# Layer two's attention: output weights halved ahead of the Fourier read-out, three roots behind the last exponential, zero products in waits of both layers

## The chip, the cores and the metric

The kernel runs on one core of a Trainium2 chip. Its time is the time on the device from start to end, in microseconds (us); lower is better. The engines are TensorE (PE, with its weight loads PEld), VectorE (DVE), ScalarE (ACT), GpSimd (POOL) and SyncE (SP), which issues the DMAs. Each runs its own program in order and they meet at semaphores.

## The reference, cut to what matters

The model has two parts that run one after the other on 256 tokens of width 1024. The first part has two layers of token mixers and experts; the second has four feed-forward blocks, a recurrent block and a pooling block. The change touches the token mixers of the first part:

```
for l in range(2):
    hx, hc = modulated rms_norm of x and of the context
    px, pc = hx @ w_in, hc @ w_in
    ya = chunk_spatial_gating(...)        # group 0
    yb = fourier_mix(...)                 # group 1
    yc = softmax0(q k) - lam*softmax1(q k), times v      # group 2: "c", 4 heads
    yd = softmax(q k + bias + mask), times v             # group 3: "d", 4 heads
    y  = rms_norm over each head of [ya yb yc yd], times head gain
    x  = x + g1 * (y @ w_out)
    x  = x + g2 * expert_choice_ffn(...)  # 16 experts, 12 MB of weights each
```

Layer one (l = 0) does this for the 256 tokens and the 256 of the context, layer two (l = 1) has context only as keys and values, so it has half of the query tiles.

## The kernel before, in words

Tokens lie in tiles of 128. All weights come through a ring of 7 slots of 2 MB (`ring` and `ring_top`). SP's program issues the loads in the order in which they are used; each waits until the products of the slot's former user have passed on PE (`weights_used`). Weights of ordinary projections are split: ACT copies a chunk of 128x4096 numbers to a shorter format (`halve_lead`, L390), DVE subtracts it from the chunk and keeps the rest (`halve_rest`, L398), and PE makes three products of each pair (`exact`, L747 to L749). A split chunk holds two slots. Layer two's `w_out` comes as two such chunks.

The order within a layer, written out by hand for each engine:

- projection by `w_in`, norms of q and k, transposes of q and k of "c" (`turn_qk`, L896; read by ACT in L1498 and DVE in L2009), spatial gating (DVE L1995);
- Fourier mix: products over channels (L855), ACT copies the results `uv` to SBUF (`read_fourier_uv`, L1490), in layer two PE then makes 26 products of zeros (`stay_busy`, L759, a product of 128x128 zeros by 512 columns of zeros whose result nobody reads), then products over tokens (L873), and DVE reads them (L2002);
- `attention_c`: a unit is one query tile and one head, 16 units in layer one and 8 in layer two. For each unit PE makes scores (L916), DVE the maximum (L2019), ACT the exponential (L1510), DVE combines the two maps (L2037), PE transposes them (L930), ACT copies them (`c_wt`, L1521), and PE multiplies by v (L939). Scores run three units ahead, so the last three units have no scores to issue in between;
- `turn_qk` again for "d" (L896), and `attention_d`, with the same number of units: POOL masks q (L556), PE scores, bias and mask (L956 to L961), DVE maximum (L2057), ACT exponential (L1534), PE transposes (L971), ACT copy (L1554), PE product by v (L991), DVE scaling (L2063);
- within `attention_d`'s loop, at fixed units, stand the norms of the pieces of y that are ready: ACT squares (`y_squares`, L1568), DVE sums (`y_sums`, L2092), ACT roots (`y_std`, L1576), DVE reciprocal and products (`y_norm`, L2100 and L2103). Half way through the loop stands the halving of the first chunk of `w_out`. The fourth piece is normed behind the loop;
- `merge`: router products of the shift (L1034), 2 (layer one) or 7 (layer two) zero products, PE transposes y (L1006), ACT and DVE read and split it (L1582, L2111), then the products by `w_out` for 8 tiles of 128 output features, with the router's products of each tile (`token_logits`, L1043) behind the products of the next. ACT and DVE halve the second chunk of `w_out` in the meantime;
- routing and the 16 experts (L1175, L1187, L1198).

Exponential and root lie in different tables of ACT: where the two follow each other, the trace shows an `ACT_TABLE_LOAD` on ACT.

Of the kernel before, what the change touches and what calls it, by code (L numbers as in the profile page):

```python
# [117 lines left out]
def before(name, layer):  # L118

    return COUNTS[name] * layer  # L120
# [18 lines left out]
def build(nc, dram, out_t):  # L139
    ctx = ExitStack()  # L140
    with ctx:
# [173 lines left out]
        chunk_at = {}  # L315
# [420 lines left out]
        def _(pe):  # L736
# [164 lines left out]
            def attention_c(l):  # L901
                todo = units(l)
                pe.wait_ge(sem("qk_t_act"), 2 + before("qk_t_act", l))
                pe.wait_ge(sem("qk_t_dve"), 2 + before("qk_t_dve", l))

                def scores(u):
                    q, h = todo[u]
                    lo, width = keys(q)
                    if u >= 3:
                        pe.wait_ge(sem("c_exp"), 2 * (u - 2) + before("c_exp", l))  # L910
                    if u == 2:

                        pe.wait_ge(sem("fourier_read"), (2 if l == 0 else 1) + before("fourier_read", l))
                    pe.wait_ge(sem("c_bands"), u + 1 + before("c_bands", l))
                    for m in range(2):
                        pe.matmul(ps[:, 2 * (u % 3) + m, 0:width], q_band[:, 2 * (u % 4) + m, :],  # L916
                                  qk_t[:, 2 + (2 * h + m) // 4, lo:lo + width], start=True, stop=True)\
                            .then_inc(sem("c_scores"), 1)

                for u in range(3):  # L920
                    scores(u)
                stay_busy(6, 8)
                for u, (q, h) in enumerate(todo):
                    lo, width = keys(q)
                    tiles = width // P
                    pe.wait_ge(sem("c_weights"), u + 1 + before("c_weights", l))
                    if u >= 1:
                        pe.wait_ge(sem("c_wt"), u + before("c_wt", l))
                    for j in range(tiles):
                        mm = pe.transpose(ps[:, 6, P * j:P * j + P], expo[:, 2 * (u % 3), P * j:P * j + P], ident)  # L930
                    mm.then_inc(sem("c_turned"), 1)
                    if u + 3 < len(todo):
                        scores(u + 3)
                    pe.wait_ge(sem("c_wt"), u + 1 + before("c_wt", l))
                    if h == 0 and q >= 1:
                        pe.wait_ge(sem("c_out"), q + before("c_out", l))
                    at = HEAD * h
                    for j in range(tiles):
                        mm = pe.matmul(ps[:, 7, at:at + HEAD], w_t[:, u % 2, j, :],  # L939
                                       vals[:, lo // P + j, HEAD * h:HEAD * h + HEAD], start=j == 0, stop=j == tiles - 1)  # L940
                    mm.then_inc(sem("c_pv"), 1)
# [54 lines left out]
            def merge(l):  # L996
# [11 lines left out]
                for d in range(KT):  # L1008
                    n = chunk_at["w_out", l] + d // 4
                    if d % 4 == 0:  # L1010
                        halved_chunk(n)
                    if d == 0:
                        pe.wait_ge(sem("y_rest"), KT + before("y_rest", l))
                    if d >= 6:
                        pe.wait_ge(sem("mix_added"), d - 5 + before("mix_added", l))
# [412 lines left out]
        def _(act):  # L1428
# [97 lines left out]
            def attention_d(l):  # L1526
# [11 lines left out]
                for u in range(len(todo)):  # L1538

                    if l == 0 and u in (5, 12):  # L1540
                        ada_group(3 if u == 5 else 4)
                    if u in (2, 4, 6):
                        y_std(l, u // 2 - 1)
                    if u in (0, 2, 4):
                        y_squares(l, u // 2)
                    if u == len(todo) // 2:
                        halve_lead(act, chunk_at["w_out", l])
                    if u + 1 < len(todo):
                        softmax(u + 1)
# [7 lines left out]
            def y_squares(l, piece):  # L1557
                tiles = 4 if l == 0 else 2
                lo, heads, _ = Y_PIECES[piece]

                if piece == 0:
                    act.wait_ge(sem("sgu_done"), 1 + before("sgu_done", l))
                    act.wait_ge(sem("fourier_read"), tiles // 2 + before("fourier_read", l))
                elif piece == 2:
                    act.wait_ge(sem("c_out"), tiles + before("c_out", l))
                elif piece == 3:
                    act.wait_ge(sem("d_out"), len(units(l)) + before("d_out", l))
# [241 lines left out]
            for l in range(LAYERS):  # L1809
# [19 lines left out]
                read_qk_t(l, 0)  # L1829
                if l == 0:  # L1830
                    ada_group(1)
                read_fourier_uv(l)
                attention_c(l)
                read_qk_t(l, 1)
                if l == 0:
                    ada_group(2)
                attention_d(l)
                y_squares(l, 3)
                y_std(l, 3)
                merge(l)  # L1840
# [28 lines left out]
        def _(dve):  # L1869
# [181 lines left out]
            def attention_d(l):  # L2051
# [16 lines left out]
                for u in range(len(todo)):  # L2068

                    if l == 0 and u in (7, 14):  # L2070
                        ada_group(3 if u == 7 else 4)
                    if u in (3, 5, 7):
                        y_norm(l, u // 2 - 1)
                    if u in (1, 3, 5):
                        y_sums(l, u // 2)
                    if u == len(todo) // 2:
                        halve_rest(dve, chunk_at["w_out", l])
                    if u + 2 < len(todo):
                        maximum(u + 2)
# [459 lines left out]
            for l in range(LAYERS):  # L2539
# [18 lines left out]
                spatial_gating(l)  # L2558
                if l == 0:
                    ada_group(1)  # L2560
                read_fourier(l)
                attention_c(l)
                read_qk_t(l, 1)
# [1 line left out]
                    ada_group(2)  # L2565
                attention_d(l)
                gains(l, 1)
                y_sums(l, 3)
                y_norm(l, 3)
                merge(l)  # L2570
                route(l)
# [192 lines left out]
```

## Time and profile before

| | us |
|---|---|
| median of 3 runs | 2490.08 |
| lowest, highest | 2489.24, 2499.73 |
| profiled execution, its time | 2492.37 |
| profiled execution, its span | 2490.6 |

| engine | busy us | share of the span |
|---|---|---|
| PE | 2253.0 | 90% |
| PEld | 1485.7 | 60% |
| DVE | 1129.9 | 45% |
| ACT | 846.7 | 34% |
| POOL | 52.9 | 2% |

The DMA moved 660.62 MB at a mean of 265 GB/s. The mean granted clock of TensorE was 0.986 of its full speed of 2.4 GHz; its other level is 1.2 GHz. Busy time says how long an engine worked, not whether the end waited for it: that is read from who released whom. In the rows a time is the start counted from the start of the span, "x8" says that eight instructions were merged in one row, and the bracket at the end says how long the engine had been idle before it and which instruction released it. In the trace layer one's first attention ends near 210 and its merge starts near 279; layer two's first attention runs from 931 to 965, its second from 968 to 1002, and its merge begins near 1006. The experts of layer two follow from about 1061.

### The profile page before, as it was taken

How to read it: one execution, taken by the hardware profiler on the slowest of the kernel's cores; microseconds unless marked ns; L12 is line 12 of the kernel's file. 1: busy time of each engine (PE TensorE's matmuls, PEld its weight loads, DVE VectorE, ACT ScalarE, POOL GpSimd, SP SyncE). 2: the span in 40 equal slices, each digit the busy share in tenths (PEclk: the TensorE clock that was granted, in tenths of full speed). 3: DMA queues.
4: the chain of work that ended last, by engine and by line, in shares of the span. 5: the costliest groups of instructions: out<-in, count | busy, mean ns of one | idle time of the engine just before them, and what ended most of it. 6: DMA issues, size and time to landing. Idle time of an engine off the chain costs nothing.

```text
span 2490.6 us, 28697 instructions
## 1 busy us (share of the span) xinstructions
PE 2253.0 (90%) x12159; PEld 1485.7 (60%) x12159; DVE 1129.9 (45%) x1652; ACT 846.7 (34%) x1200; POOL 52.9 (2%) x88
## 2 busy tenths in 40 slices
PE   6999999889787898898787879999999999999997
PEld 3865773324232585722131216889998888877887
DVE  5535551102010655511010006758877668568755
ACT  4435421001000435310000005544755466435544
POOL 0022000000000001000000000000000000010000
PEclk9999999999999998999999999999999999999999
DMA  7375369999999450389999997445354454353442
GB/s 321 119 300 210 129 271 418 427 428 427 429 428 427 176 198 1 136 376 428 428 427 428 427 428 287 167 163 224 119 215 170 182 199 186 127 220 135 182 161 85
DMA packets 64047, 660.62 MB, mean 265 GB/s; under 512 B 7152, under 2 KB 9200, under 8 KB 20144
## 3 DMA queue, kind: packets, MB, share of 16 engines
q1 hardware_dynamic: 63776, 658.27, 64.9%
q8 instruction: 96, 1.57, 0.3%
q10 hardware_dynamic: 144, 0.52, 0.1%
q14 instruction: 31, 0.25, 0.0%
HBM read 657.71 MB, written 1.05 MB: 265 GB/s over the span
## 4 chain that ended last, share of the span: by engine, by line
PE 66%; DMA 24%; DVE 6%; ACT 3%; issue 1%; SPq 0%; POOL 0%; DVEq 0%; ACTq 0%; POOLq 0%
PE ps L777 20%; PE ps L778 10%; DMA ring<-in_exp_up 8%; PE ps L1175 7%; DMA ring_top<-in_exp_up 6%; PE ps L747 4%; PE ps L748 4%; PE ps L749 4%; PE ps L1198 4%; DMA ring_top<-in_exp_gate 3%; DMA ring<-in_exp_gate 2%; DMA ring_top<-in_exp_down 2%; PE ps L1149 1%; PE ps L800 1%; PE ps L916 1%
## 5 line engine op out<-in xcount | busy, mean ns | idle before, releaser
L1175 PE MATMUL ps<-ring,arena 128*32 128x512 f32 (+1 forms) x1184 | 265.8, 595 | 56.3 <-DMA ring<-in_exp_up 29.0
L777 PE MATMUL ps<-h_buf_r,ring_r 128*128 128x512 f32 x800 | 284.1, 400 | 3.7 <-DVE h_buf_r L636 3.7
L2261 DVE TENSOR_TENSOR h_buf<-h_buf,ps 128x512 f32<-128x512 f32 (+1 forms) x32 | 21.9, 683 | 505.4 <-PE ps L1175 505.4
L1175 PE MATMUL ps<-ring_top,arena 128*64 128x512 f32 (+1 forms) x864 | 194.7, 595 | 44.1 <-DMA ring_top<-in_exp_up 23.9
L778 PE MATMUL ps<-h_buf_r,ring_r 128*128 128x256 f32 x800 | 224.7, 281 | 0.0
L1175 PEld LDWEIGHTS ps<-ring,arena 128*32 128x32 f32 (+1 forms) x1184 | 72.8, 122 | 245.4 <-issue 147.1
L777 PE MATMUL ps<-h_buf_r,ring_top_r 128*128 128x512 f32 x608 | 216.3, 400 | 2.9 <-DVE h_buf_r L636 2.9
L398 DVE TENSOR_TENSOR ring_r<-ring,ring_r 128x2048 fp32r<-128x2048 f32 (+4 forms) x83 | 172.5, 2117 | 66.4 <-ACT ring_r L390 66.3
L777 PEld LDWEIGHTS ps<-h_buf_r,ring_r 128*128 128x128 f32 x800 | 151.0, 189 | 41.5 <-issue 4.5
L778 PE MATMUL ps<-h_buf_r,ring_top_r 128*128 128x256 f32 x608 | 170.9, 281 | 0.0
L1175 PEld LDWEIGHTS ps<-ring_top,arena 128*64 128x64 f32 (+1 forms) x864 | 53.7, 124 | 182.7 <-issue 106.0
L2271 DVE COPY arena<-ps 32x512 f32<-32x512 f32 x48 | 33.1, 689 | 270.1 <-PE ps L1198 269.9
L778 PEld LDWEIGHTS ps<-h_buf_r,ring_r 128*128 128x128 f32 x800 | 151.6, 190 | 0.1
L390 ACT ACTIVATE ring_r<-ring 128x2048 fp32r<-128x2048 f32 (+4 forms) x83 | 142.7, 1765 | 0.0
L1198 PE MATMUL ps<-ring,h_buf 128*64 128x512 f32 (+1 forms) x560 | 126.3, 596 | 15.0 <-ACT h_buf L1634 10.3
L398 DVE TENSOR_TENSOR ring_top_r<-ring_top,ring_top_r 128x2048 fp32r<-128x2048 f32 (+3 forms) x57 | 121.6, 2171 | 34.3 <-ACT ring_top_r L390 34.3
L777 PEld LDWEIGHTS ps<-h_buf_r,ring_top_r 128*128 128x128 f32 x608 | 115.0, 189 | 31.1 <-issue 3.0
L777 PE MATMUL ps<-arena_r,ring_r 128*128 128x512 f32 x352 | 124.2, 397 | 0.0
L1634 ACT ACTIVATE h_buf<-ps 128x512 f32<-128x512 f32 (+1 forms) x32 | 15.7, 490 | 307.8 <-PE ps L1187 307.8
L778 PEld LDWEIGHTS ps<-h_buf_r,ring_top_r 128*128 128x128 f32 x608 | 115.4, 190 | 0.1
L1198 PE MATMUL ps<-ring_top,h_buf 128*32 128x512 f32 (+1 forms) x464 | 104.5, 596 | 11.3 <-ACT h_buf L1634 8.6
L1639 ACT ACTIVATE arena<-ps 32x512 f32<-32x512 f32 x48 | 28.2, 587 | 240.9 <-PE ps L1198 240.7
(341 smaller groups left out, 4284.5 us busy)
## 6 DMA issues: line engine op xcount, KB each, us to landing
ring<-in_exp_gate SPq DMA_DIRECT2D x39, 2048.0 KB, 28.7
ring<-in_exp_down SPq DMA_DIRECT2D x35, 2048.0 KB, 29.8
ring<-in_exp_up SPq DMA_DIRECT2D x35, 2048.0 KB, 30.5
ring_top<-in_exp_up SPq DMA_DIRECT2D x29, 2048.0 KB, 30.5
ring_top<-in_exp_down SPq DMA_DIRECT2D x29, 2048.0 KB, 29.6
ring_top<-in_exp_gate SPq DMA_DIRECT2D x25, 2048.0 KB, 30.2
ring<-in_ffn_w SPq DMA_DIRECT2D x50, 1024.0 KB, 6.8
ring_top<-in_ffn_w SPq DMA_DIRECT2D x38, 1024.0 KB, 6.9
```

Source lines behind the costliest of these rows:

```text
L390: act.activation(halves(n)[0][:, at], slot(n)[:, at], ACT.Copy).then_inc(sem("chunk_lead"), 1)
L398: dve.tensor_tensor(rest, slot(n)[:, at], lead, ALU.subtract).then_inc(sem("chunk_halved"), 1)
L747: release(pe.matmul(out, a[0], b[0], start=start, stop=False, skip_group_check=True))
L748: pe.matmul(out, a[0], b[1], start=False, stop=False, skip_group_check=True)
L749: return pe.matmul(out, a[1], b[0], start=False, stop=stop, skip_group_check=True)
L777: release(pe.matmul(ps[:, bank, :], w[0][:, lo:lo + P], both, start=start, stop=False, skip_group_check=True))
L778: return pe.matmul(ps[:, bank, 0:N], w[1][:, lo:lo + P], both[:, 0:N], start=False, stop=stop, skip_group_check=True)
L800: mm = pe.matmul(ps[32 * j:32 * j + 32, 7, :], cond[:, k, :], slot(n + k // 2)[:, at:at + 512], start=k == 0, stop=k == KT - 1)
L1175: mm = pe.matmul(ps[half * m:half * m + m, which, :], xe[:, k, :], slot(c)[:, at:at + 512], start=k == 0, stop=k == KT - 1)
L1198: mm = pe.matmul(ps[half * m:half * m + m, 3, :], hid_t[:, k % 4, k // 4, :], slot(c)[:, at:at + 512], start=k == 0, stop=k == KT - 1)
L1639: ins = act.activation((o_lat, o_ctx)[s][32 * j:32 * j + 32, 0:512], ps[32 * s:32 * s + 32, 3, :], ACT.Copy)
L2271: ins = dve.tensor_copy((o_lat, o_ctx)[s][32 * j:32 * j + 32, 512:1024], ps[m + 32 * s:m + 32 * s + 32, 3, :])
```

## The change

In layer two, the halving of the first chunk of `w_out` moves from the middle of `attention_d` to the place before ACT's and DVE's read-out of the Fourier mix. Also in layer two, the roots and the norms of the first three pieces of y move from `attention_d`'s loop behind it: ACT makes the three roots ahead of the squares of the last piece; DVE does the first norm ahead of the last sums and the other two behind them. `y_squares` now waits until the sums of the piece before it were made, in both layers. PE gets zero products in both layers: three in each of the last three units of `attention_c`, between the transposes and the wait for ACT's copy, and seven in `merge` ahead of the wait for the last split piece of y, before the first products by `w_out`.

```diff
--- before.py
+++ after.py
@@ -931,6 +931,8 @@
                     mm.then_inc(sem("c_turned"), 1)
                     if u + 3 < len(todo):
                         scores(u + 3)
+                    else:
+                        stay_busy(2 * (u % 3), 3)
                     pe.wait_ge(sem("c_wt"), u + 1 + before("c_wt", l))
                     if h == 0 and q >= 1:
                         pe.wait_ge(sem("c_out"), q + before("c_out", l))
@@ -1010,6 +1012,7 @@
                     if d % 4 == 0:
                         halved_chunk(n)
                     if d == 0:
+                        stay_busy(6, 7)
                         pe.wait_ge(sem("y_rest"), KT + before("y_rest", l))
                     if d >= 6:
                         pe.wait_ge(sem("mix_added"), d - 5 + before("mix_added", l))
@@ -1539,11 +1542,11 @@
 
                     if l == 0 and u in (5, 12):
                         ada_group(3 if u == 5 else 4)
-                    if u in (2, 4, 6):
+                    if l == 0 and u in (2, 4, 6):
                         y_std(l, u // 2 - 1)
                     if u in (0, 2, 4):
                         y_squares(l, u // 2)
-                    if u == len(todo) // 2:
+                    if l == 0 and u == len(todo) // 2:
                         halve_lead(act, chunk_at["w_out", l])
                     if u + 1 < len(todo):
                         softmax(u + 1)
@@ -1558,6 +1561,8 @@
                 tiles = 4 if l == 0 else 2
                 lo, heads, _ = Y_PIECES[piece]
 
+                if piece:
+                    act.wait_ge(sem("y_sums"), piece + before("y_sums", l))
                 if piece == 0:
                     act.wait_ge(sem("sgu_done"), 1 + before("sgu_done", l))
                     act.wait_ge(sem("fourier_read"), tiles // 2 + before("fourier_read", l))
@@ -1829,12 +1834,17 @@
                 read_qk_t(l, 0)
                 if l == 0:
                     ada_group(1)
+                else:
+                    halve_lead(act, chunk_at["w_out", l])
                 read_fourier_uv(l)
                 attention_c(l)
                 read_qk_t(l, 1)
                 if l == 0:
                     ada_group(2)
                 attention_d(l)
+                if l:
+                    for piece in range(3):
+                        y_std(l, piece)
                 y_squares(l, 3)
                 y_std(l, 3)
                 merge(l)
@@ -2069,11 +2079,11 @@
 
                     if l == 0 and u in (7, 14):
                         ada_group(3 if u == 7 else 4)
-                    if u in (3, 5, 7):
+                    if l == 0 and u in (3, 5, 7):
                         y_norm(l, u // 2 - 1)
                     if u in (1, 3, 5):
                         y_sums(l, u // 2)
-                    if u == len(todo) // 2:
+                    if l == 0 and u == len(todo) // 2:
                         halve_rest(dve, chunk_at["w_out", l])
                     if u + 2 < len(todo):
                         maximum(u + 2)
@@ -2558,6 +2568,8 @@
                 spatial_gating(l)
                 if l == 0:
                     ada_group(1)
+                else:
+                    halve_rest(dve, chunk_at["w_out", l])
                 read_fourier(l)
                 attention_c(l)
                 read_qk_t(l, 1)
@@ -2565,7 +2577,12 @@
                     ada_group(2)
                 attention_d(l)
                 gains(l, 1)
+                if l:
+                    y_norm(l, 0)
                 y_sums(l, 3)
+                if l:
+                    y_norm(l, 1)
+                    y_norm(l, 2)
                 y_norm(l, 3)
                 merge(l)
                 route(l)
```

## Rows read from the trace of the kernel before

**Rows 1.** The page, part 4: chain that ended last, share of the span by engine.

```profile
PE 66%; DMA 24%; DVE 6%; ACT 3%; issue 1%; SPq 0%; POOL 0%; DVEq 0%; ACTq 0%; POOLq 0%
```

**Rows 2.** Stretches: length, busy per engine (count), clock, DMA share, GB/s.

```profile
955.00:973.00 18.00, 15.01 (x55) 11.45 (x54) 3.09 (x6) 3.62 (x8) 4.66 (x8) 0.53 0.01 1
...
1070.00:1500.00 430.00, 352.35 (x1610) 98.51 (x1604) 33.63 (x60) 25.91 (x50) 0.00 (x0) 1.00 1.01 428
```

**Rows 3.** Timeline of SP's queue, 820 to 1075: start, length, issue.

```profile
878.64 11.23 SPq L459 DMA_DIRECT2D ring_top<-in_w_out  x2
...
1026.81 0.33 SPq L459 DMA_DIRECT2D ring_top<-in_exp_up  x1
```

**Rows 4.** Timeline of ACT and DVE, layer two's second attention.

```profile
985.08 3.60 ACT L390 ACTIVATE ring_top_r<-ring_top 128x4096 fp32r<-128x4096 f32 x1
...
988.70 1.28 ACT L1534 ACT_TABLE_LOAD   x1
...
997.97 0.69 ACT L1534 ACTIVATE arena<-ps,small 128x512 f32<-128x512 f32 x1
...
988.72 4.43 DVE L398 TENSOR_TENSOR ring_top_r<-ring_top,ring_top_r 128x4096 fp32r<-128x4096 f32 x1 [3.10 <-ACT ring_top_r L390]
```

**Rows 5.** Timeline, 915 to 932: start, length, engine, line [idle before <-releaser].

```profile
918.39 0.60 ACT L1498 ACTIVATE arena<-ps 128x512 f32<-128x512 f32 x1 [0.27 <-PE ps L896]
...
921.53 5.78 PE L759 MATMUL ps<-zeros 128*128 128x512 bf16 x26
...
930.79 0.69 DVE L2002 COPY arena<-ps 128x512 f32<-128x512 f32 x1 [9.94 <-PE ps L873]
```

**Rows 6.** Timeline of PE, layer two's second attention.

```profile
975.41 1.07 PE L991 MATMUL ps<-arena 128*128 128x64 f32 x8
...
978.22 1.00 PE L991 MATMUL ps<-arena 128*128 128x64 f32 x8
...
990.83 1.12 PE L971 MATMUL ps<-const,arena 128*128 128x128 f32 x4 [3.60 <-ACT arena L1534]
...
996.64 1.00 PE L991 MATMUL ps<-arena 128*128 128x64 f32 x8
```

**Rows 7.** Timeline of DVE and PE, between attention and merge, layer two.

```profile
1001.32 0.28 DVE L2063 TENSOR_SCALAR arena<-ps,small 128x64 f32<-128x64 f32 x1 [0.54 <-PE ps L991]
...
1004.15 0.76 DVE L2103 TENSOR_TENSOR arena<-arena,small 128x256 f32<-128x256 f32 x2
...
1005.72 2.55 PE L1006 MATMUL ps<-const,arena 128*128 128x128 f32 x16
```

**Rows 8.** Timeline of PE, end of layer two's first attention.

```profile
917.26 1.53 PE L896 MATMUL ps<-const,arena 128*128 128x128 f32 x12 [0.47 <-ACT arena L1453]
...
953.59 1.08 PE L939 MATMUL ps<-arena 128*128 128x64 f32 x8 [1.42 <-DVE arena L2027]
...
955.80 1.97 PE L939 MATMUL ps<-arena 128*128 128x64 f32 x8 [0.69 <-ACT arena L1521]
...
957.56 1.06 PE L930 MATMUL ps<-const,arena 128*128 128x128 f32 x4
...
964.58 2.77 PE L896 MATMUL ps<-const,arena 128*128 128x128 f32 x12
...
968.28 2.04 PE L956 MATMUL ps<-arena 128*128 128x512 f32 x2 [0.94 <-POOL arena L556]
```

**Rows 9.** Timeline of PE, layer one.

```profile
206.00 0.66 PE L939 MATMUL ps<-arena 128*128 128x64 f32 x4 [0.47 <-ACT arena L1521]
...
209.98 3.62 PE L896 MATMUL ps<-const,arena 128*128 128x128 f32 x16
...
287.25 0.47 PE L747 MATMUL ps<-h_buf_r,ring_r 128*128 128x512 f32 x1 [2.54 <-DVE arena_r L2111]
```

**Rows 10.** Timeline of PE, first products of layer two's merge.

```profile
1010.27 0.36 PE L747 MATMUL ps<-h_buf_r,ring_top_r 128*128 128x256 f32 x1 [2.00 <-DVE arena_r L2111]
...
1018.22 0.62 PE L1043 MATMUL ps<-router_sb,arena 128*128 128x16 f32 x4 [1.97 <-DVE arena L2133]
```

## The prediction

> **What bounds the kernel now.** I read the chain that ended last first: TensorE (PE) holds 66% of the span and DMA 24% [rows 1]. The stretches say where each holds. In layer two's experts the DMA moves 428 GB/s at a share of 1.01; in the end of its first attention the DMA share is 0.01 and the granted clock is 0.53, so half of full speed or 1.2 GHz nearly throughout [rows 2]. The queue of SP explains the silence: `w_out` goes out from 878.64, and the next weights that are held back by a full ring leave at 1026.81, when the merge's first half has used its weights [rows 3]. So the attention of layer two is bounded by a serial chain of PE, ACT and DVE, and whatever time it gives back starts the expert stream earlier by the same amount. The stream itself becomes no longer and no shorter. I therefore count one for one up to the end.
>
> **1. Halving moved ahead of the Fourier read-out (layer two).** ACT's copy to the lead half takes 3.60 us and DVE's subtraction 4.43 us [rows 4]. They now stand behind the reads of the turned q and k. ACT's last such read starts at 918.39 and lasts 0.60, so the copy runs from 919.0 to 922.6, and the two reads of `uv` (about 0.6 each) end near 923.9. PE doesn't look at them before its 26 zero products end near 927.1 (921.53 and 26 by 0.216) [rows 5]: 3.2 us of cover. DVE subtracts from 922.6 to 927.1 and has to be free at 930.79, where it had been idle for 9.94 us [rows 5]: 3.7 us of cover. The `w_out` weights were issued from 878.64 on [rows 3], 40 us earlier. Cost 0; no DMA is issued by a moved step and nothing is put ahead of SP's queue, since ring slots come free by PE's products. If the cover were gone, the cost would be the part of 3.60 that sticks out. Range 0 to 3.6 loss, value 0, by rows 5.
>
> **2. What goes from the second attention (layer two).** Before, PE waited 3.60 us for one exponential [rows 6], which stood behind the copy of 3.60 and a table load of 1.28; DVE then took 4.43 us for the rest [rows 4]. Three roots also stood between exponentials, with two table loads each. An undisturbed unit lasts 2.81 us (975.41 to 978.22), and the products of unit 5 start at 996.64 [rows 6]. Undisturbed they would start at 975.41 + 5 x 2.8 = 989.4: gain 7.2. That includes 5 us which PE spent at half speed because of the pause (the 4 transposes at 990.83 show 1.12 [rows 6]; at full speed such a group lasts 0.6). Behind it the last exponential, at 997.97, still waited for its table [rows 4]; its maximum was there 0.8 earlier: gain 0.8. Next late is the ordinary chain of PE: scores 1.45, transposes 0.43, products 0.84 to 0.9, which is the unit of 2.8; ACT needs some 2.1 us of it with its squares and DVE 1.8.
>
> **3. The tail (layer two).** Before, DVE's last scaling ended at 1001.60; the last normalised piece was there at 1004.91, that is 3.3 later, but PE began to transpose only at 1005.72, 4.1 later, because its seven zero products at half speed ran over [rows 7]. Now ACT does a table load (1.28) and three roots (0.2 each in steady issue) after its last copy, which is about 0.5 us longer than the last scaling takes; the square of the last piece comes 0.5 later, its root then needs no load. DVE has one `y_norm` before the last sums, hidden by that wait, and two behind them: each a short reciprocal and the 0.76 of two products [rows 7], 0.9 together. So y is ready 3.3 + 1.4 = 4.7 after the last scaling and PE starts at 4.85: loss 0.7. PE's zero products end long before. Ends: 0.3 gain (DVE hides all) to 2 loss (all three behind the sums); 0.7 is the sum by the order of the program.
>
> The row has 1.28 for a load [rows 4]. The Trainium skill (ScalarE: Activation LUTs, What ACT_TABLE_LOAD costs) asks about 2.66 us for every switch, drain included, which no row here shows. By it the one switch in the tail would push the last sums 1.4 further, and the total below would be 14.3 instead of 15.7.
>
> **4. Zero products at the end of the first attention, both layers.** Units 5, 6 and 7 get three each; one costs 0.216 at full and 0.43 at half speed, so 0.65 or 1.3, in a wait for ACT of 0.69 [rows 8]. Before, PE idled 1.42 and then 0.69 [rows 8], and from 955.8 on 8 products took 1.97 instead of 1.08, 4 transposes 1.06 instead of 0.6 and the 12 of the next turn 2.77 instead of 1.53 [rows 8]. From 955.80 to 964.58 lie two units of 3.51 and the last products, 1.76. If full speed holds, a unit is 0.88 of products, 0.44 of transposes and the wait of 0.69, so 2.0, twice: gain 3.0; the last products 0.9; the turn 1.24. Together 5.1. The gap of 1.42 is still there, so the clock may fall once more; but PE then has no gaps, and before it rose near 972 after PE had worked without one from 968.28 on, where it had stayed low through gaps of 0.69. So I expect few slow us, with zeros at half speed: a gain of about 3.6. I take 4.4. Up to 972 PE also ran slow in the first scores of the second attention (3.7 us from 968.28 [rows 2, 8]); half of that, 1.8, comes on top.
> In layer one the same wait is 0.47 [rows 9], so each group sticks out by 0.18 at full speed, 0.5 in all, and by 0.8 each at half speed. There the 16 transposes took 3.62 at 209.98 [rows 9]; at 0.1275 each (1.53 for 12 [rows 8]) they take 2.04: gain 1.6; the last two units and the first `ada` products give another 1.1. Net 2.2. Behind it layer one is PE and a DMA that PE's releases start, so it passes on. Range for the clock's share of both layers: from 4 loss (all zeros at half speed) to 9.6 gain.
>
> **5. Seven zero products before the merge's products.** They cost 1.5 us at full speed, in gaps of 2.00 (layer two) [rows 10] and 2.54 (layer one) [rows 9]: 0. At half speed 3.0, so 0.5 late in layer one, while in layer two PE stops a second time for 1.97 at 1018.22 for DVE's second halving [rows 10], which hides it. A gain isn't shown either: the second stop stays. Value 0, range -1 to +1.5. The new wait before the squares for the sums has long been met: the old root needed the same sums.
>
> **Sum.** 7.2 + 0.8 - 0.7 + 4.4 + 1.8 + 2.2 = 15.7 us. The profiled execution took 2492.37 (span 2490.6 and 1.8 around it), so its like would take 2476.7; on the median of 2490.08 that is 2474.4.
>
> **Rivals.**
> A. *Only half of the clock comes back.* The stalls of parts 2 and 3 give 7.3; the clock 3 to 5 instead of 8.4, because it falls once in each tail, or because the executions differ in where it falls. For: the gap of 1.42 stays, and a new idle of 1.8 us comes before the transposes. 11 us: 2479. Against: PE has no other gap of note.
> B. *Zero products don't hold the clock.* 8.0 - 0.7 - 1.8 (layer two, 3 x 0.6) - 2.4 (layer one) - 0.5 = 2.6: 2487.5. For: they stand in the tail behind a real gap. Against: after the 26 zeros the clock is full.
> C. *The time is absorbed.* If the expert stream were bound by something that doesn't start with the merge, nothing would come through: 2490. Against: SP's queue shows a release by the merge [rows 3], and an idle DMA [rows 2].
> D. *The moved halving holds the Fourier stage (slower).* The reads of `uv` stand behind ACT's copy, which waits for `w_out` and for its slot. It decides once the copy starts later than 918.99 + 3.2, and makes the kernel slower once it starts more than 3.2 + 15.7 = 19 us late, at 938; at 30 us late it gives 2501. Against: the issue at 878.64 [rows 3].
>
> **How the numbers follow.** Forecast 0.66, A 0.20, B 0.07, C 0.04, D 0.03. Predicted is the forecast's 2474.4. Its own range is 2471 to 2477.5. The range 2468 to 2482 adds the upper bounds of parts 4 and 5 (some 5 more) below and takes in A above. A measurement here tells about 0.5% or 12.5 us from no change. Faster by more than that (below 2477.6): the forecast and a fourth of A, 0.71. Within: the rest of A, B and C, 0.26. Slower 0.03.
>
> **What would show it.** Part 1: ACT's copy near 919 and a first Fourier product right behind the 26 zeros, as before; else it is wrong. Part 2: eight units at 2.8 us without a pause of PE, no table load between exponentials. Part 3: one load and three roots behind the last copy; PE idle 1.5 to 2 us before the transposes, which start 4.85 after the last scaling. Part 4: granted clock near 1 from 940 to the end of the second attention but for one short fall, and the turn of 12 in 1.5 us. Part 5: no move of the first product of the merge against the last transposes. The forecast is wrong if the second attention's units stay above 3 us, or if the clock stays near 0.5 where rows 2 has 0.53.

## The result, and the profile after

The changed kernel took 2475.56 us (median of 6 runs, 2469.26 to 2478.42), the kernel before 2490.02 (6 runs): a ratio of 0.9928 with the interval 0.9912 to 0.9945, so 14.5 us less, faster beyond doubt but by less than 1%. Forecast were 2474.4 and 15.7 less. The profiled execution took 2473.89 (span 2472.1) against 2492.37 (2490.6), 18.5 less; its granted clock is 0.991 on the mean against 0.986.

The chain that ended last is nearly what it was [rows 1], PE and DMA, on the page of the changed kernel:

```profile
span 2472.1 us, 28757 instructions
...
PE 67%; DMA 23%; DVE 6%; ACT 3%; issue 1%; SPq 0%; DVEq 0%; POOL 0%; ACTq 0%; POOLq 0%
```

The stretches of the changed kernel (length, busy time of PE, weight load, DVE, ACT and POOL, granted clock, DMA share, GB/s), to be held against [rows 2]:

```profile
949.00:960.00 11.00, 9.05 (x66) 6.90 (x65) 4.59 (x13) 4.33 (x9) 0.57 (x1) 1.00 0.01 1
960.00:984.00 24.00, 22.97 (x142) 17.55 (x142) 10.63 (x29) 13.39 (x30) 4.09 (x8) 1.00 0.00 1
1002.00:1004.00 2.00, 2.00 (x12) 2.00 (x11) 0.00 (x0) 0.00 (x0) 0.00 (x0) 0.50 0.00 0
1053.00:1480.00 427.00, 349.58 (x1598) 98.11 (x1596) 33.45 (x60) 25.05 (x49) 0.00 (x0) 1.00 1.01 428
```

Where the clock was 0.53 with an idle DMA, it is now 1.00 (full speed, 2.4 GHz), through the end of the first attention and the whole second one. In the merge, at 1002, it is at half for a moment. The experts move the same 428 GB/s as before.

PE's timeline of the changed kernel, layer two from the Fourier products to the merge, with two rows of layer one ahead (start, length, engine, line, operation, [idle before <- what ended it]):

```profile
206.05 0.65 PE L941 MATMUL ps<-arena 128*128 128x64 f32 x4
...
209.25 1.92 PE L896 MATMUL ps<-const,arena 128*128 128x128 f32 x16
...
918.41 5.78 PE L759 MATMUL ps<-zeros 128*128 128x512 bf16 x26
924.03 3.62 PE L873 MATMUL ps<-arena,h_buf 128*128 128x256 f32 x16
...
950.49 1.08 PE L941 MATMUL ps<-arena 128*128 128x64 f32 x8 [1.42 <-DVE arena L2037]
951.40 0.60 PE L930 MATMUL ps<-const,arena 128*128 128x128 f32 x4
951.84 0.81 PE L759 MATMUL ps<-zeros 128*128 128x512 bf16 x3
...
957.17 1.10 PE L941 MATMUL ps<-arena 128*128 128x64 f32 x8
958.11 1.48 PE L896 MATMUL ps<-const,arena 128*128 128x128 f32 x12
960.52 1.10 PE L958 MATMUL ps<-arena 128*128 128x512 f32 x2 [0.94 <-POOL arena L556]
...
966.09 1.00 PE L993 MATMUL ps<-arena 128*128 128x64 f32 x8
...
979.75 1.00 PE L993 MATMUL ps<-arena 128*128 128x64 f32 x8
...
983.39 2.11 PE L1037 MATMUL ps<-router_sb,mod 128*128 128x16 f32 x16
985.34 3.15 PE L759 MATMUL ps<-zeros 128*128 128x512 bf16 x7
988.44 2.35 PE L1008 MATMUL ps<-const,arena 128*128 128x128 f32 x16
...
992.71 0.38 PE L747 MATMUL ps<-h_buf_r,ring_top_r 128*128 128x256 f32 x1 [0.40 <-DVE arena_r L2121]
...
1000.75 0.51 PE L1046 MATMUL ps<-router_sb,arena 128*128 128x16 f32 x3 [2.03 <-DVE arena L2143]
```

1. *Tail of the first attention* (950.49 on, was 953.59 [rows 8]): the gap of 1.42 is still there, but the 8 products behind it take 1.10 at most and the 4 transposes 0.60; the zeros take 0.81 (0.65 steady). The turn of 12 takes 1.48 instead of 2.77. From the first of these products to the turn: 10.99 before, 7.62 now.
2. *Second attention*: scores at 960.52, first products at 966.09, those of unit 5 at 979.75, which is five units of 2.73 without a pause of PE; before, the pause of 3.60 lay in them [rows 6].
3. *Behind it*: seven zero products at half speed (3.15) end at 988.49, and the transposes start there. The merge's first product starts at 992.71, the logits' first at 1000.75 after 2.03 of waiting, as before [rows 10].
4. *Layer one*: the turn of 16 takes 1.92 instead of 3.62 [rows 9].

ACT, DVE and SP of the changed kernel, in three timelines: the moved halving, the roots behind the last copy, the last scaling, and the release of the expert weights:

```profile
915.74 3.61 ACT L390 ACTIVATE ring_top_r<-ring_top 128x4096 fp32r<-128x4096 f32 x1
919.25 1.07 ACT L1493 ACTIVATE arena<-ps 128x512 f32<-128x512 f32 x2
...
981.76 0.60 ACT L1557 ACTIVATE arena<-ps 128x512 f32<-128x512 f32 x1 [0.26 <-PE ps L973]
982.38 1.28 ACT L1581 ACT_TABLE_LOAD   x1
983.67 0.68 ACT L1581 ACTIVATE small<-small,eps_col 128x8 f32<-128x8 f32 x3
...
919.38 4.57 DVE L398 TENSOR_TENSOR ring_top_r<-ring_top,ring_top_r 128x4096 fp32r<-128x4096 f32 x1 [1.68 <-ACT ring_top_r L390]
927.68 0.69 DVE L2012 COPY arena<-ps 128x512 f32<-128x512 f32 x1 [3.72 <-PE ps L873]
...
983.59 0.28 DVE L2073 TENSOR_SCALAR arena<-ps,small 128x64 f32<-128x64 f32 x1 [0.54 <-PE ps L993]
...
987.63 0.76 DVE L2113 TENSOR_TENSOR arena<-arena,small 128x256 f32<-128x256 f32 x2
...
1009.31 0.33 SPq L459 DMA_DIRECT2D ring_top<-in_exp_up  x1
```

SP's release of the experts' weights comes at 1009.31; it was at 1026.81 [rows 3]. All that layer one and the attention of layer two give back arrives there: 17.5 us, and the span is 18.5 shorter.

### The profile page after: what moved, and what is told of

It is laid out like the page before. It is cut to its first block, busy times and chain, and to the rows that moved or that the text cites. A ratio compares the mean times of both kernels' runs of the same rounds, so it can differ in the third digit from the quotient of the medians.

```text
span 2472.1 us, 28757 instructions
## 1 busy us (share of the span) xinstructions
PE 2251.1 (91%) x12191; PEld 1481.9 (60%) x12191; DVE 1130.5 (46%) x1652; ACT 838.7 (34%) x1194; POOL 56.8 (2%) x88
## 4 chain that ended last, share of the span: by engine, by line
PE 67%; DMA 23%; DVE 6%; ACT 3%; issue 1%; SPq 0%; DVEq 0%; POOL 0%; ACTq 0%; POOLq 0%
PE ps L777 20%; PE ps L778 10%; PE ps L1178 8%; DMA ring<-in_exp_up 7%; DMA ring_top<-in_exp_up 6%; PE ps L747 4%; PE ps L748 4%; PE ps L749 4%; PE ps L1201 4%; DMA ring_top<-in_exp_gate 3%; DMA ring_top<-in_exp_down 2%; DMA ring<-in_exp_gate 2%; PE ps L1152 1%; PE ps L800 1%; PE ps L916 1%; DMA ring<-in_exp_down 1%
## 5 line engine op out<-in xcount | busy, mean ns | idle before, releaser
L398 DVE TENSOR_TENSOR ring_r<-ring,ring_r 128x2048 fp32r<-128x2048 f32 (+4 forms) x83 | 172.5, 2118 | 64.8 <-ACT ring_r L390 64.7
L398 DVE TENSOR_TENSOR ring_top_r<-ring_top,ring_top_r 128x2048 fp32r<-128x2048 f32 (+3 forms) x57 | 121.8, 2174 | 34.7 <-ACT ring_top_r L390 34.7
L1639 ACT ACTIVATE h_buf<-ps 128x512 f32<-128x512 f32 (+1 forms) x32 | 15.7, 490 | 305.7 <-PE ps L1190 305.7
```

The source lines that it names most:

```text
L398: dve.tensor_tensor(rest, slot(n)[:, at], lead, ALU.subtract).then_inc(sem("chunk_halved"), 1)
```

## Experiments

Each kernel is the changed one with the edit shown (`-` lines leave the changed kernel), except where it says otherwise. All ratios are against the kernel before, measured beside it on the same chip (medians 2490.89 us for e1 to e4, 2489.77 for e5 to e8, 2490.90 for f1 to f4). The time from one instruction to another within layer two's attention serves for reading the profiles, since it doesn't depend on where an execution lost time elsewhere: *P to T*, from the fifth of the eight groups of products at the end of the first attention (953.59 before, 950.49 changed) to the transposes behind the second attention, is 52.13 before and 37.95 changed.

**e1_no_zeros**: both groups of zero products out.

```
-                    else:
-                        stay_busy(2 * (u % 3), 3)
-                        stay_busy(6, 7)
```

> The changed kernel without any of its new zero products (none at the end of the first attentions, none ahead of the merges' products); halving and roots stay moved. My theory (two parts that add: stalls 7.3 us, clock 8.4 us): 7.3 us under the kernel before, about 2483; in its profile layer two's second attention has units of 2.8 us, the end of its first attention is at half speed as before (12 transposes in 2.77), and the second attention's first scores are slow. Rival 1 (the gain is the clock's, the stalls only made it fall): no more than 3 us under before, 2487 or more. Rival 2 (the stalls' part includes the clock's, zeros are ornament): 12 us or more under before, 2478 or less.

Measured: 2479.57 (7 runs), ratio 0.9954 [0.9937, 0.9972]; P to T 42.06. PE's timeline has the half speed back in the tail, as [rows 8] had it, but full speed by the first scores:

```profile
956.76 1.76 PE L939 MATMUL ps<-arena 128*128 128x64 f32 x8 [0.69 <-ACT arena L1521]
...
965.33 2.43 PE L896 MATMUL ps<-const,arena 128*128 128x128 f32 x12
968.69 1.10 PE L956 MATMUL ps<-arena 128*128 128x512 f32 x2 [0.94 <-POOL arena L556]
```

The reordering of ACT and DVE alone gives 11.3 us on the medians (7.3 were expected), of which P to T shows 10.1: 2.1 up to the first products of the second attention (at 974.26) and 8.0 behind them.

**e2_zeros_only**: the kernel before with only the two groups of zero products added.

> The kernel before with only the new zero products (three in each of the last three units of both first attentions, seven ahead of each merge's products); halving and roots stay where they were. My theory: 8.4 us under before, about 2481.5, and it adds up with the run without zeros to the change's 14.5 within some 2 us; the profile shows full clock through the end of the first attention and a pause of 3.6 us with a slow stretch still in the second attention of layer two. Rival (zeros don't hold the clock): no gain or up to 3 us loss against what the wait hides, 2488 to 2490. Rival 2 (zeros are worth nothing without the stalls gone, because the clock falls again in the pause): at most 4 us under before.

Measured: 2483.27 (12 runs), 0.9971 [0.9954, 0.9988], so 7.6 less; P to T 49.25. This profiled execution was the longest of its kernel, by time lost elsewhere (1468.2 from SP's release to the end, 1463.8 before), so only stretches of the attention are read from it. PE's timeline shows why P to T gains so little: the tail is as short as in the changed kernel, but the stop for the halving is still there, and half speed comes back behind it:

```profile
984.57 0.66 PE L973 MATMUL ps<-const,arena 128*128 128x128 f32 x4 [3.60 <-ACT arena L1537]
...
993.12 3.57 PE L993 MATMUL ps<-arena 128*128 128x64 f32 x16
```

The two halves sum to 18.9 on the medians, each with an interval of some 4 us to either side. That is 4.4 more than the 14.5 of the changed kernel's first runs and about the 19.4 of its second ones (f1 below); in P to T they sum to 13.0 of 14.2. So they add up to the change within the noise, and neither is idle.

**e3_no_end_zeros**: only the groups of three out.

```
-                    else:
-                        stay_busy(2 * (u % 3), 3)
```

> The changed kernel without the zero products in the last three units of the first attentions; the seven ahead of the merge's products stay. My theory: the end zeros are worth 8.4 of the 14.5, so about 6 us under before, 2484, the same as the run without any zeros within 1 us. Rival (the merge's zeros carry part of the clock's gain): 3 us or more better than the run without any zeros.

Measured: 2481.62 (11 runs), 0.9964 [0.995, 0.9979], 9.3 less than before where 6 were expected; P to T 42.05, as without any zeros (e1). PE's timeline: the fifth group of products, the second attention's first scores, the transposes behind it.

```profile
953.71 1.08 PE L939 MATMUL ps<-arena 128*128 128x64 f32 x8 [1.42 <-DVE arena L2035]
...
967.84 1.10 PE L956 MATMUL ps<-arena 128*128 128x512 f32 x2 [0.94 <-POOL arena L556]
...
995.76 2.35 PE L1006 MATMUL ps<-const,arena 128*128 128x128 f32 x16 [1.62 <-DVE arena L2111]
```

From the products to the first scores it takes 14.13, the changed kernel 10.03: the groups of three are worth 4.1 in layer two, all of it in the tail. **e4_no_merge_zeros**: only the groups of seven out.

```
-                        stay_busy(6, 7)
```

> The changed kernel without the seven zero products ahead of the merge's products, in both layers; the end zeros stay. My theory: they are worth 0 (range 1 us loss to 1.5 us gain), so this kernel takes what the changed one takes, about 2475.5, within 1.5 us. Rival (they keep the clock up for the merge's products): 2 us or more slower than the changed kernel, with a slow stretch at the merge's start. Rival 2 (they only stand in the way where they run at half speed): 1 to 2 us faster.

Measured: 2474.73 (6 runs), 0.9935 [0.9912, 0.9957]; P to T and the merge's start as in the changed kernel. So the groups of three carry what the zeros give (6 to 7 us on the medians between e3 and e4, or e3 and the changed kernel; 4.1 of it in layer two's tail, and in layer one PE's transposes behind the `ada` products start at 218.89 in the changed kernel and 222.22 in e3), and the groups of seven nothing that can be measured.

**e5_halving_moved_only**: the halving stays moved, roots and scalings go back into the loop.

```
-                    if l == 0 and u in (2, 4, 6):
+                    if u in (2, 4, 6):
                         y_std(l, u // 2 - 1)
...
-                    if l == 0 and u in (3, 5, 7):
+                    if u in (3, 5, 7):
                         y_norm(l, u // 2 - 1)
```

(and the calls behind `attention_d` out)

> The changed kernel with the three roots and norms back in the loop of layer two's second attention; the halving stays ahead of the Fourier read-out and the zero products stay. My theory: each of the three roots holds one exponential for two table loads (2.6 us) of which PE's unit of 2.7 hides all but about 1 us, so units 2, 4 and 6 are 0.8 to 1.0 longer, together 2.8, and the tail is 0.5 shorter: 2.3 us slower than the changed kernel, so 12.5 under before (2478.4). Rival (the roots are the larger part of the stall): 5 us or more slower than the changed kernel. Rival 2 (the clock falls in the short waits too): 5 us or more slower, with a stretch at half speed in the second attention.

Measured: 2474.91 (10 runs), 0.9935 [0.9914, 0.9955]; P to T 39.43, 1.5 more than changed. **e6_roots_moved_only** is the other half: the halving goes back to the middle of the loop, the roots stay behind.

```
-                    if l == 0 and u == len(todo) // 2:
+                    if u == len(todo) // 2:
                         halve_lead(act, chunk_at["w_out", l])
...
-                else:
-                    halve_lead(act, chunk_at["w_out", l])
```

(the same in DVE's program with `halve_rest`)

> The changed kernel with the halving back in the middle of layer two's second attention; the roots stay behind the last exponential and the zero products stay. My theory: one pause remains, ACT's 3.60 less about 1.4 of slack, then a maximum behind DVE's 4.43, 4 to 5 us together, and 0 to 3 us of half speed after it: 4 to 8 us slower than the changed kernel (2480 to 2483). Rival (the halving hides, the roots made the stall): less than 2 us slower than the changed kernel.

Measured: 2484.10 (12 runs), 0.9975 [0.9956, 0.9995]; P to T 45.42. PE's timelines, first with the roots in the loop (e5), then with the halving there (e6):

```profile
975.74 0.66 PE L973 MATMUL ps<-const,arena 128*128 128x128 f32 x4 [0.84 <-ACT arena L1537]
...
987.30 0.66 PE L973 MATMUL ps<-const,arena 128*128 128x128 f32 x4 [1.37 <-ACT arena L1537]
```

```profile
981.58 0.66 PE L973 MATMUL ps<-const,arena 128*128 128x128 f32 x4 [1.31 <-ACT arena L1537]
...
986.79 0.66 PE L973 MATMUL ps<-const,arena 128*128 128x128 f32 x4 [2.15 <-ACT arena L1537]
...
989.82 3.51 PE L993 MATMUL ps<-arena 128*128 128x64 f32 x16
```

With the roots in the loop PE stops for 0.84 and 1.37 and keeps its speed. With the halving there it stops for 1.31 and 2.15, and the last 16 products run at half speed (3.51, against 1.99 in the changed kernel). The halving was the stall. With it gone, the roots in the loop cost 1.5 in the profile and nothing on the medians (2474.91 beside 2475.56); with it still in the loop, moving the roots out gives 3.8 in the profile (49.25 in e2, 45.42 here) and nothing that the medians show.

**f1_changed_again** (no edit), **f2_six_end_zeros** (`stay_busy(2 * (u % 3), 6)`) and **f3_one_end_zero** (`..., 1)`) ask how many zero products the tail wants.

> The changed kernel itself, unchanged, on the same chip as the runs beside it, since its first interval (0.9912 to 0.9945) is as wide as the parts it is compared with. Expected 14 to 16 us under before, 2475.

Measured: 2471.54 (6 runs), 0.9931 [0.9908, 0.9954], 19.4 less than before: the same program, 4 us from its first median.

> The changed kernel with six zero products instead of three in each of the last three units of both first attentions. My theory (a zero product costs its stream time once the wait for ACT is full: 0.216 us each at full speed): 2 layers x 3 units x 3 x 0.216 = 3.9 us slower than the changed kernel, seen as units of 2.9 instead of 2.24 in layer two. Rival (three don't hold the clock in every execution, six do): less than 1.5 us slower, or faster.

Measured: 2477.25 (7 runs), 0.9948 [0.9928, 0.9967], 5.7 more than f1.

> The changed kernel with one zero product instead of three in each of the last three units of both first attentions. My theory (the clock falls only where PE's idle time adds up; a third of the wait filled is too little): between the changed kernel and the one without end zeros, 3 to 5 us slower than the changed kernel, with 1 to 2 fast units before the fall. Rival (any activity in the wait is enough): the same as the changed kernel, and in layer one 0.5 us faster since nothing sticks out of the wait.

Measured: 2478.07 (12 runs, 2470.93 to 2490.78), 0.9951 [0.9934, 0.9968]. PE's timelines of the tail, six and then one:

```profile
957.15 1.46 PE L759 MATMUL ps<-zeros 128*128 128x512 bf16 x6
958.45 1.00 PE L941 MATMUL ps<-arena 128*128 128x64 f32 x8
```

```profile
954.77 0.38 PE L759 MATMUL ps<-zeros 128*128 128x512 bf16 x1
955.62 1.10 PE L941 MATMUL ps<-arena 128*128 128x64 f32 x8 [0.47 <-ACT arena L1524]
```

Six zeros stick out of the wait: a unit takes 2.57 to 2.65 instead of 2.24, the tail 1.0 more in layer two and 1.5 in layer one. A unit of 2.9 was expected, as if three zeros had filled the wait; but from the point where zeros can start (0.44 behind the transposes' start) to the next products lie 0.85, which holds nearly four. The profile shows 2.5 of the 5.7; the rest is within the noise of the medians. One zero leaves 0.47 of the wait idle, and in this execution held the clock as well as three. The mean granted clock of every run adds to what one profile shows. The kernels that halve early and have three or six (changed, f1, f2, e4, e5) show 0.989 to 0.993 in all of their 35 runs. Without the groups of three, e1 and e3 have 0.984 to 0.989. With one, 7 runs have 0.989 to 0.991 and take 2470.9 to 2478.9, and 5 have 0.985 to 0.988 and take 2480.4 to 2490.8. The likely reading is that one zero holds the clock in some executions and not in others, while three held it in all that were run. It is not shown: none of the five slower runs of f3 has a trace, the ranges touch at 0.989, the clock is a mean over the whole program, and it does not explain every spread (a run of f2 took 2485.25 at 0.989).

**e7_second_chunk_early**: the second half of `w_out` is halved early too, ACT's part before `attention_c`, DVE's before the last read-out there, so that the merge does not stop for it.

```
+                if l:
+                    halve_lead(act, chunk_at["w_out", l] + 1)
                 attention_c(l)
...
+                if l:
+                    halve_rest(dve, chunk_at["w_out", l] + 1)
                 read_out(todo[-1][0])
```

(and the merge's own two calls under `if l == 0`)

> The changed kernel with layer two's second chunk of w_out halved early as well: ACT's copy behind the read of uv, DVE's subtraction in its idle time ahead of the last read-out of the first attention. It stood between the read of the transposed y and the first residual addition (3.67 and 4.42 us in a row), which held PE for 2.03 us. My theory: that wait goes, and the first additions come 7 us earlier, so 2.0 us faster than the changed kernel, 3.5 if the slow stretch behind the wait goes too: 2472 to 2473.5. Rival (the moved subtraction delays the last read-out and the turn of q and k): 0 or slower than the changed kernel. Rival 2 (the reads of uv come too late): the first Fourier token products start later than the zeros' end.

Measured: 2471.17 (7 runs), 0.9921 [0.9894, 0.9949], 18.6 less than before. **e8_and_read_out_first** adds that DVE reads out a finished group before it takes the next maxima, in both layers:

```
+                    (read_out(q - 1) and its condition, moved up)
                     if u + 3 < len(todo):
                         maxima(u + 3)
```

> The kernel before it in this call, and in both layers' first attention DVE reads out a query tile's result ahead of the next maxima instead of behind them. PE waited for that read-out 1.42 us once in layer two and about 1.15 to 1.4 three times in layer one. My theory: these waits go or fall under 0.5, 3 to 4.5 us faster than the kernel with the second chunk early: about 2469. Rival (the maxima, now later, hold the exponentials and so the next unit): within 1 us of it.

Measured: 2464.79 (6 runs), 0.9903 [0.9873, 0.9933], 6.4 less than e7 on the medians and 2.7 less in the profiled span, where 3 to 4.5 were expected. **f4_best_without_merge_zeros** is e8 without the groups of seven.

> The kernel with the second chunk halved early and the read-out ahead of the maxima, without the seven zero products ahead of the merge's products in both layers. My theory: they are worth 0 to 1 us, so within 1.5 us of that kernel, 2464 to 2465. Rival (with the second wait in the merge gone the zeros hold the clock for its products): 2 us slower or more.

Measured: 2464.21 (4 runs), 0.9892 [0.9871, 0.9914], 26.7 less than before: the lowest median, but not to be told from e8. PE's timelines, e7 at the merge and e8 in the tail of the first attention:

```profile
994.57 0.39 PE L747 MATMUL ps<-h_buf_r,ring_top_r 128*128 128x256 f32 x1 [0.40 <-DVE arena_r L2126]
...
1000.42 0.52 PE L1046 MATMUL ps<-router_sb,arena 128*128 128x16 f32 x4
```

```profile
950.60 1.00 PE L941 MATMUL ps<-arena 128*128 128x64 f32 x8
...
952.84 1.11 PE L941 MATMUL ps<-arena 128*128 128x64 f32 x8 [0.15 <-ACT arena L1524]
```

In e7 the stop of 2.03 at the logits is gone: from the transposes to them 10.11 instead of 12.31. In e8 the gap of 1.42 at the end of the first attention is gone too, in which PE had waited for DVE's read-out. The gap stood in layer one as well; its turn starts at 206.39 instead of 209.25, and at 208.84 in e7.

## Why the prediction came out right, step by step

Milestones of PE and SP in both profiles give each term of the sum (gain in us, before less after):

| step | predicted | profile |
|---|---|---|
| layer one, and to the tail in layer two (953.59 to 950.49) | 2.2 | 3.1 |
| part 4, tail and turn of the first attention | 4.4 | 4.7 |
| part 4, first scores of the second attention | 1.8 | 1.6 |
| part 2, five units (21.23 to 13.66) | 7.2 | 7.6 |
| part 2, last exponential (4.96 to 4.12) | 0.8 | 0.8 |
| part 3, last scaling to transposes (4.12 to 4.57) | -0.7 | -0.45 |
| part 5, transposes to the merge's first product | 0 | 0.3 |
| from there to the end of the program | 0 | 0.9 |
| sum | 15.7 | 18.5 |

The agreement of the medians (2475.56 beside 2474.4) is luck in part: a second set of runs of the same program gave 2471.54. The first row holds some luck too. In layer one itself 2.9 are gained (PE's transposes behind the `ada` products start at 221.80 before, at 218.89 now). The term was 0.7 short: its zeros were priced to stick out by 0.5 and don't (units of 1.34 to 1.36 with them, 1.33 and 1.35 without), and the turn of 16 took 1.92 where 2.04 was reckoned. That the 2.9 arrives in layer two is seen in this pair of profiles and not in all: in the seven profiles with three zeros and the old read-out, those transposes start within 0.5 us of one another, but the fifth group of products starts anywhere from 950.49 (this one) to 954.10 (e5), against 953.59 before.

*Part 1* cost nothing: the Fourier product starts at 924.03, right behind the 26 zeros, with ACT's copy at 915.74 (all that part of the program is 3.1 earlier, and the copy 0.2 more). DVE was still idle for 3.72 before its read-out. Rival D has no place in the rows.

*Part 2* is right in size and, by e5 and e6, in its main cause. The prediction did not split the 7.2 between halving and roots; the runs do: of the 11.3 that P to T loses from e2 to the changed kernel, moving the halving alone gives 9.8 and moving the roots alone 3.8. With the halving gone, the roots with their table loads (two of 1.28 each time) stand mostly in ACT's slack. Some 0.4 of the 7.6 is a unit of 2.73 where 2.8 was reckoned.

*Part 3*: y is ready 4.5 after the last scaling (983.87 to 988.39), when the last of DVE's four norms is done; 4.7 were predicted. The only table load near is the one at 982.38, behind ACT's last copy, with three roots in 0.68 after it. The load took 1.28 and the first root began 1.29 after it, so the drain for which one sentence of the prediction gave the Trainium skill's figure (ScalarE: Activation LUTs, What ACT_TABLE_LOAD costs) does not show here: by that price the transposes would stand near 989.8, and they stand at 988.44. PE was not idle ahead of them, as the prediction had it. Its seven zero products ran at half speed and ended at 988.49, which happened to be the moment y was there. In f1, the same program, they ran at full speed, and the predicted idle time shows:

```profile
990.15 2.35 PE L1008 MATMUL ps<-const,arena 128*128 128x128 f32 x16 [1.62 <-DVE arena L2113]
```

P to T is 37.96 there and 37.95 in the changed kernel's profile, so y sets the start and the slow zeros cost nothing.

*Part 4* is right as a mechanism in the tail: e3 and e4 show that the groups of three hold the clock and are worth some 6 us with layer one, e1 that without them the half speed returns. Its unit was taken too short, 2.0 instead of 2.24 ([rows 8] had one at full speed, 953.59 to 955.80, 2.21): from the transposes' start to the next products pass 1.29 (951.40 to 952.69), not 0.44 + 0.69, since at full speed the transposes' own latency of 0.60 counts and not the distance at which others follow them. The error was covered by the doubt about one more fall of the clock in this tail, for which 0.7 had been set aside; the clock did not fall there. So that 4.4 is so near 4.7 is luck, two errors that cancel. The 1.6 of the first scores is not shown to come from the zeros: e1 and e3, without them, take the same 5.57 from the first scores to the first products (7.13 before), as their clock was back at full speed by then.

*Part 5* is right: no move, and e4 confirms that the groups of seven give nothing that can be measured. They do not hold the clock of the merge either. At 1002 it is at half in the changed kernel (the row above), and from the transposes to the second logits lie 17.2 there, in e2 17.3 and in the kernel before 17.1; in e1, e3 and e4 it is 15.7. f1, the same program as the changed kernel, has 15.7 too. Where in the merge the clock falls differs between executions.

*Rival A* (half the clock back, 11 us) describes e1's and e3's size, but not this kernel's runs. *Rival B* would be e1, 2479.6: the reordering alone gave 11.3 instead of the 2.6 it priced. It counted the zeros as a loss of 4.7 on top, which e1 doesn't have; without that it stands at 7.3, and behind the first products of the second attention e1 gains 8.0. The other 2.1 in P to T lie ahead of them: in e1 and e3 the half speed begins a little later than in the kernel before and is over by the first scores (968.69 in e1), while before it lasted to about 972 [rows 2]. The stalls that the reordering takes out come after that moment, so they are not shown to be its cause; it may be a difference between executions. *Rival C* falls by SP's release, 17.5 earlier, and a span 18.5 shorter.

Left open: the medians of one program differ by 4 us between two sets of runs (2475.56 and 2471.54), so the split of the 14.5 to 19 us into reordering (11.3) and zeros (6 to 7.6) is good to some 4 us each, and the last 0.9 of the table is not assigned. Much of the spread lies behind SP's release, where these kernels run the same program: from there to the end of the span it takes 1463.8 before and 1462.8 in the changed kernel, but 1457.1 in e5 and 1468.2 in e2.

## What to carry to other kernels

Where a DMA-bound stretch follows a latency-bound one, ask which instruction releases the DMA queue, and count every microsecond ahead of it once; this held to 1 us in 18 in the pair of profiles, while the stretch behind the release differs by up to 11 us between profiles, so medians of several runs are needed to see it. Work with long instructions (here a copy of 3.6 and a subtraction of 4.4) belongs where its engine already waits, not between the links of a chain of 2.8 us units; short ones (roots with their loads) can stay once the long ones are gone. A wait that recurs in every unit can be filled with products on zeros of just its length: too many lengthen the unit, too few probably hold the clock only in some executions, and the mean clock of all runs is a second witness where one profile looks good.

## What had not been expected of the hardware

GpSimd slowed beside DVE's subtraction. POOL's timeline, its 8 band products, first of the kernel before, then of the changed one:

```profile
918.99 4.66 POOL L545 TENSOR_SCALAR arena<-arena,const 128x128 f32<-128x128 f32 x8 [669.04 <-ACT arena L1498]
```

```profile
915.84 8.58 POOL L545 TENSOR_SCALAR arena<-arena,const 128x128 f32<-128x128 f32 x8 [668.80 <-ACT arena L1501]
```

The same 8 instructions took 4.66 and then 8.58, 3.9 more, beside DVE's L398 at 919.38 (4.57), which reads two operands from SBUF. Taken one by one, seven of them last 0.60 each, also beside ACT's copy, and the last, begun at 919.89 while the subtraction ran, lasts 4.53 and ends at 924.42, 0.5 behind the subtraction's end at 923.95. In e6, where the roots moved and the halving did not, the 8 take 4.65; in e1, e5 and f1, with the halving early, 8.59 or 8.60. PE's next scores start at 927.48, so it cost nothing. The Trainium skill (SBUF — State Buffer, "SBUF: two separate sides") says that DVE and GpSimd share one pair of ports under a lock held for a whole instruction, and that DVE's operations with two SBUF inputs take it against a GpSimd operation that reads SBUF; the trace agrees, with one GpSimd instruction of 0.60 that took 4.53 beside a subtraction of 4.57. Where the subtraction stood before, at 988.72 [rows 4], POOL had nothing to do.

PE's speed fell for a moment though it had not paused since 981.07: its products of 16 columns at 983.39 are followed at once by zeros at half speed (985.34, 0.45 each). f1, the same program, has a granted clock of 1.00 from 985 to 1000, so this too differs between executions.

PE's clock did not fall in the changed kernel after an idle 1.42 at 949.1, with the zeros behind it, and was at half in e1 after the same gap with idles of 0.69 behind it. So in these two executions it was not the one gap alone that decided; what came after it differed.
